# State-space scan of a hybrid decoder step: decay differences by one 48-row product, step sizes folded into the inputs, fills placed by hand

## The reference

```python
cum = cumsum(dt * a)                              # per head, within the block (a < 0)
seg = cum[i] - cum[j]                             # per head, i >= j
lmat = where(mask, exp(where(mask, seg, 0)), 0)
cb = einsum('bign,bjgn->bgij', C, B)
scores = cb * lmat * dt[j]
y = einsum('bghij,bjghp->bighp', scores, x) + einsum(C, state) * exp(cum)[..., None]
wts = exp(cum[last] - cum) * dt
state = state * exp(cum[last]) + einsum('bjgn,bjgh,bjghp->bghpn', B, wts, x)
```

## Time and profile before

| | |
|---|---|
| median of three executions | 3562.12 us |
| profiled execution | 3558.76 us, span of the core 3557.2 us, mean TensorE clock 0.919 of full |
| TensorE busy | 3054.7 us (86%) |
| VectorE busy | 1840.0 us (52%) |
| ScalarE busy | 1210.5 us (34%) |
| GpSimd busy | 519.1 us (15%) |
| DMA | 448.18 MB, mean 126 GB/s |

### The profile page before, as it was taken

How to read it: one execution, slowest core, us unless ns; L and a number is a source line. 1 busy time by engine, 2 the same in 40 slices (tenths; PEclk the granted TensorE clock), 3 DMA queues, 4 the chain that set the end, 5 groups by cost and what they waited for, 6 DMA issues and landing times. The chain is left out here.

```text
span 3557.2 us, 63864 instructions
## 1 busy us (share of the span) xinstructions
PE 3054.7 (86%) x25660; PEld 2801.4 (79%) x25660; DVE 1840.0 (52%) x2858; ACT 1210.5 (34%) x1641; POOL 519.1 (15%) x339
## 2 busy tenths in 40 slices
PE   8999888877786998799889998888787778987997
PEld 7998788677575988599889897776675758975997
DVE  4435545584565554344344364555854654643443
ACT  4436321132131443244254363111411214432542
POOL 0005510252220000000000055002422100000000
PEclk9999999887897999999999999998877979999998
DMA  4444410333272555344344444002422624553443
GB/s 157 151 128 144 125 49 3 72 122 107 67 272 83 172 172 194 125 130 148 114 138 148 127 144 132 25 24 70 153 68 76 254 105 162 183 172 138 134 148 104
DMA packets 119406, 448.18 MB, mean 126 GB/s; under 512 B 13616, under 2 KB 23888, under 8 KB 111632
## 3 DMA queue, kind: packets, MB, share of 16 engines
q1 hardware_dynamic: 97920, 329.75, 29.2%
q0 software_dynamic: 21264, 115.34, 8.9%
HBM read 397.01 MB, written 48.02 MB: 125 GB/s over the span
## 5 line engine op out<-in xcount | busy, mean ns | idle before, releaser
L842 PE MATMUL gemm_banks<-in_high,w_high 128*128 128x320 f32 (+1 forms) x2864 | 856.4, 314 | 61.9 <-ACT w_high L1406 33.4
L1406 ACT ACTIVATE w_high<-ring 128x1024 fp32r<-128x1024 f32 x598 | 631.8, 1057 | 745.6 <-PE gemm_banks L846 373.9
L843 PE MATMUL gemm_banks<-in_low,w_high 128*128 128x320 f32 (+1 forms) x2864 | 845.0, 310 | 0.0
L1770 DVE TENSOR_TENSOR w_low<-ring,w_high 128x1024 fp32r<-128x1024 f32 x436 | 532.7, 1222 | 497.8 <-ACT w_high L1406 497.7
L842 PEld LDWEIGHTS gemm_banks<-in_high,w_high 128*128 128x128 f32 x2864 | 548.1, 191 | 71.6 <-issue 63.7
L693 POOL TENSOR_TENSOR w_low<-ring,w_high 128x1024 fp32r<-128x1024 f32 x162 | 411.8, 2547 | 1047.6 <-ACT w_high L1406 793.7
L843 PEld LDWEIGHTS gemm_banks<-in_low,w_high 128*128 128x128 f32 x2864 | 548.0, 191 | 2.7
L846 PE MATMUL gemm_banks<-in_high,w_low 128*128 128x320 f32 (+1 forms) x2864 | 475.0, 308 | 6.2 <-POOL w_low L693 4.0
L846 PEld LDWEIGHTS gemm_banks<-in_high,w_low 128*128 128x128 f32 x2864 | 431.4, 189 | 8.9 <-POOL w_low L693 5.4
L899 PE MATMUL gemm_banks<-in_high,w_high 128*128 128x320 f32 x640 | 218.5, 353 | 33.7 <-ACT stage L1474 13.7
L926 PE MATMUL gemm_banks<-act_high,w_high 128*128 128x320 f32 x704 | 215.0, 318 | 3.3 <-DVE arena L1819 3.3
(11 more groups left out here) (381 smaller groups left out, 4297.0 us busy)
## 6 DMA issues: line engine op xcount, KB each, us to landing
ring<-in_w SPq DMA_DIRECT2D x598, 512.0 KB, 3.5
arena<-in_kc POOLq DMA_DIRECT2D x16, 1024.0 KB, 6.5
arena<-in_vc POOLq DMA_DIRECT2D x16, 1024.0 KB, 8.9
out_fill<-stage SPq DMA_DIRECT2D x80, 160.0 KB, 3.9
arena<-out_fill POOLq DMA_DIRECT2D x4, 2560.0 KB, 12.1
arena<-in_ssm POOLq DMA_DIRECT2D x16, 512.0 KB, 10.4
out_s_ssm<-arena POOLq DMA_DIRECT2D x16, 512.0 KB, 7.0
arena<-in_ret POOLq DMA_DIRECT2D x16, 512.0 KB, 24.5
```

Source lines behind the costliest of these rows:

```text
L842: mm(dst, w_high[:, slot, w(k)], in_high[:, k, 0:n], start=(k == 0), stop=False)
L843: mm(dst, w_high[:, slot, w(k)], in_low[:, k, 0:n], start=False, stop=False)
L1406: f(w_high[:, slot], ring[:, s, 0:D], ACT.Copy).then_inc(weights_high, 1)
L1770: tt(w_low[:, slot], ring[:, pos % RING, 0:D], w_high[:, slot].bitcast(F32), ALU.subtract).then_inc(weights_split, 1)
```

## The change

- The decay differences come from one product per quarter, straight into PSUM: the stationary operand `one_cum` has 48 rows (16 of ones, 16 of zeros, 16 with the cumulative decay), and the moving operand `cumd` holds the diagonal in rows 0 to 15 and the negated identity, spread over 128 columns, in rows 32 to 47. The clamp goes from four VectorE instructions to one ScalarE instruction (`Relu` with scale -1, followed by `Exp` with scale -1).
- The step size is multiplied into x (`xdt`) as it is copied from PSUM, on VectorE; the score is then one multiplication over four heads. `xw` too is made straight from PSUM. ScalarE no longer copies x, and copies B instead.
- TensorE's order is new: 4 fills per block instead of 5 (and 4 in the third block as before, between other steps), the read of the state ahead of quarters 2 and 3, the update ahead of the turning back, y turned back into banks 3 and 6. After the blocks, the first sample update, the sum of squares, and then the other sample updates with a fill after each.
- The silu of z moves from ahead of the scan into the third block. The gate comes ahead of the samples' updates, and the final scaling between the fourth and the fifth; the projection for retention waits for the last update instead of `done`. The mask of C for the samples (`Cm`) moves to the end of the second block.
- VectorE prepares `one_cum` by three small instructions during the convolution, and ScalarE writes the negated identity at the head of the scan.

```diff
+        one_cum = dts[0:48, 4]
...
                 for t, b in enumerate(IN_PAIRS):
+                    if t == NS // 2:
+                        pool.wait_ge(ss["V"].sem, ss["V"].value["done"])
+                        pool.dma_start(outs["ssd"], rb).then_inc(dma["ssd_stored"][0], 16)
                     pool.wait_ge(ss["V"].sem, ss["V"].value[("updated", t)])
                     n += save(outs["s_ssm"][l, b], ssS[:, b])
-
-                pool.wait_ge(ss["V"].sem, ss["V"].value["done"])
-                pool.dma_start(outs["ssd"], rb).then_inc(dma["ssd_stored"][0], 16)
...
-                    need(V, "tok") if tb == 0 else need(V, (tb - 1, "state"))
+                    if tb == 0:
+                        need(cv_a, CB - 1)
+                        need(V, "tok")
+                    else:
+                        need(V, (tb - 1, "y"))
...
-                    fill("fill_ssd", 1)
-                    need(V, (tb, "tr"))
...
+
+                def cum(tb, q):
+                    c0, n = TBS[tb]
+                    if q < 2:
+                        need(V, (tb, "cumd"))
+                        need(A, "negated") if tb == 0 else need(V, (tb - 1, "state"))
+                    else:
+                        need(A, (tb, "exp", q - 2))
+                    here = bank(4 + q % 2)[0:n, :].rearrange("p (a b) -> p a b", b=P)[:, :, 0:n]
+                    hit(mm(here, one_cum[:, c0:c0 + n], cumd[0:48, 4 * q:4 * q + 4, 0:n], start=True, stop=True),
+                        M, (tb, "cum", q))
+
+                def y(tb, q):
+                    n = TBS[tb][1]
+                    need(V, (tb, "score", q))
+                    if tb and q == 0:
+                        need(V, (tb - 1, "yf"))
+                    for j in range(4):
+                        hd = 4 * q + j
+                        ins_ = mm(bank((3, 6)[q // 2])[0:n, (hd % 8) * 64:(hd % 8 + 1) * 64], sco[0:n, q % 2, j, 0:n],
+                                  xdt[0:n, hd * 64:(hd + 1) * 64], start=True, stop=True)
+                    hit(ins_, M, (tb, "y", q))
...
+                def update(tb):
+                    n = TBS[tb][1]
+                    need(A, (tb, "exp", 3))
+                    for g in range(2):
+                        ins_ = mm(bank(4 + g)[:, 0:512], btok[0:n, g], xw[0:n, g * 512:(g + 1) * 512],
+                                  start=True, stop=True)
+                    hit(ins_, M, (tb, "update"))
...
-                        ins_ = tr(bank(k // 4)[:, (k % 4) * P:(k % 4) * P + n], ytok[0:n, k * P:(k + 1) * P],
+                        ins_ = tr(bank((3, 6)[k // 4])[:, (k % 4) * P:(k % 4) * P + n], ytok[0:n, k * P:(k + 1) * P],
...
+                fill("fill_ssd", 1)
+                for tb in range(3):
+                    turn(tb)
+                    fill("fill_ssd", 1)
+                    cum(tb, 0)
+                    cum(tb, 1)
+                    fill("fill_ssd", 1)
+                    y(tb, 0)
+                    cum(tb, 2)
+                    y(tb, 1)
+                    cum(tb, 3)
+                    fill("fill_ssd", 1)
+                    read(tb)
+                    y(tb, 2)
+                    y(tb, 3)
                     if tb < 2:
...
+                        update(tb)
+                    fill("fill_ssd", 1)
+                    turn_back(tb)
+                fill("fill_ssd", 1)
+                sample_update(0)
+                fill("fill_ssd", 1)
+                for k in range(KT):
+                    if k == 0:
+                        need(A, "sq")
+                    ins_ = mm(bank(6)[:, 0:T], K("ones"), z[:, k, :], start=(k == 0), stop=(k == KT - 1))
+                hit(ins_, M, "sum")
+                for j in range(1, 4):
+                    sample_update(j)
+                    fill("fill_ssd", 1)
+                fill("fill_ssd", 20 - filled["fill_ssd"])
                 need(V, ("updated", NS - 1))
-                fill("fill_ssd", 20 - filled["fill_ssd"])
-                sums(M, "sum", K("ones"), lambda k: z[:, k, :], T, [(A.sem, A.value["sq"])])
-                need(V, "done")
...
                 silus(1 + CB)
-                arrived(act_, layer, "z_back")
-                A_.mark(f(z, z, ACT.Silu), A, "z")
...
             def ssd():
                 V, A, M = ss["V"], ss["A"], ss["P"]
+                need(cv_v, CB - 1)
+                A_.mark(f(cumd[32:48], each(K("ident", 32, 48)[:, 32:48], P), ACT.Copy, scale=-1.0), A, "negated")
                 fill("fill_ssd", 1)
                 for tb, (c0, n) in enumerate(TBS):
-                    need(M, (tb, "tr"))
-                    A_(f(xtok[0:n, 0:512], bank(0)[0:n, 0:512], ACT.Copy))
-                    A_.mark(f(xtok[0:n, 512:1024], bank(1)[0:n, 0:512], ACT.Copy), A, (tb, "tr"))
                     fill("fill_ssd", 1)
                     for q in range(4):
-                        need(V, (tb, "seg", q))
-                        A_.mark(f(seg[0:n, q % 2, :, 0:n], seg[0:n, q % 2, :, 0:n], ACT.Exp), A, (tb, "exp", q))
-                        if q in (0, 2):
+                        if q == 2:
+                            need(V, (tb, "tr"))
+                            A_.mark(f(btok[0:n], bank(2)[0:n, 0:2 * P].rearrange("p (a b) -> p a b", b=P), ACT.Copy), A, (tb, "tr"))
+                        need(M, (tb, "cum", q))
+                        if q >= 2:
+                            need(V, (tb, "score", q - 2))
+                        here, s = bank(4 + q % 2)[0:n, :].rearrange("p (a b) -> p a b", b=P)[:, :, 0:n], seg[0:n, q % 2, :, 0:n]
+                        A_(f(s, here, ACT.Relu, scale=-1.0))
+                        A_.mark(f(s, s, ACT.Exp, scale=-1.0), A, (tb, "exp", q))
+                        if q % 2:
                             fill("fill_ssd", 1)
-                    fill("fill_ssd", 2 if tb < 2 else 1)
-                fill("fill_ssd", 20 - filled["fill_ssd"])
+                    if tb == 2:
+                        arrived(act_, layer, "z_back")
+                        A_.mark(f(z, z, ACT.Silu), A, "z")
+                    fill("fill_ssd", 1)
+                fill("fill_ssd", 2)
                 need(V, "gate")
                 A_.mark(f(z, xc[:, 0:8], ACT.Square), A, "sq")
                 need(M, "sum")
-                rsqrt(sroot, mp[:, 0, 0:T], sinv, A, "root")
+                rsqrt(sroot, bank(6)[:, 0:T], sinv, A, "root")
+                fill("fill_ssd", 20 - filled["fill_ssd"])
...
+                V_(nc.vector.memset(one_cum, 0.0))
+                V_(nc.vector.memset(one_cum[0:16], 1.0))
+                V_(copy(one_cum[32:48], D_(0)))
...
+                spread(0)
                 V_(nc.vector.memset(sst, 0.0))
-                need(cv_a, CB - 1)
-                for g in range(2):
-                    ins_ = tt(Cm[:, g], rep(xc[:, 10 + g, TP:T], NS), split(K("seqrow"), NS, C64), ALU.mult)
-                    V_(ins_) if g == 0 else V_.mark(ins_, V, "cm")
...
-                    V_.mark(tt(cumd[0:16, :, 0:n], rep(D_(0)[:, c0:c0 + n], 16), each(id16, n), ALU.mult), V, (tb, "cumd"))
...
-                    V_(copy(btok[0:n], bank(2)[0:n, 0:2 * P].rearrange("p (a b) -> p a b", b=P)))
...
-                    need(A, (tb, "tr"))
-                    x3, w3 = (split(v, 16, C64)[0:n] for v in (xtok, xw))
-                    V_.mark(tt(w3, x3, each(tok[0:n, tb, 3], C64), ALU.mult), V, (tb, "tr"))
...
-                        for j in range(4):
-                            ins_ = ts(seg[0:n, q % 2, j, 0:n], bank(4 + q % 2)[0:n, j * P:j * P + n],
-                                      tok[0:n, tb, 0, 4 * q + j:4 * q + j + 1], 0.0, ALU.subtract, ALU.min)
...
+                    heads8 = lambda v: v.rearrange("p (a b) -> p a b", b=C64)
+                    for g in range(2):
+                        V_(tt(heads8(xdt[0:n, g * 512:(g + 1) * 512]), heads8(bank(g)[0:n, 0:512]),
+                              each(tok[0:n, tb, 1, 8 * g:8 * g + 8], C64), ALU.mult))
+                    V_.mark(tt(cbm[0:n, :, 0:n], bank(2)[0:n, 2 * P:4 * P].rearrange("p (a b) -> p a b", b=P)[:, :, 0:n],
+                               rep(K("ssdmask", 0, n) if tb < 2 else K("s_ssdmask", 0, 64), 2), ALU.mult), V, (tb, "tr"))
+                    for g in range(2):
+                        ins_ = tt(heads8(xw[0:n, g * 512:(g + 1) * 512]), heads8(bank(g)[0:n, 0:512]),
+                                  each(tok[0:n, tb, 3, 8 * g:8 * g + 8], C64), ALU.mult)
+                        V_(ins_) if g == 0 else V_.mark(ins_, V, (tb, "xw"))
...
                         need(A, (tb, "exp", q))
                         if q >= 2:
                             need(M, (tb, "y", q - 2))
-                        for j in range(4):
-                            ins_ = stt(sco[0:n, q % 2, j, 0:n], seg[0:n, q % 2, j, 0:n],
-                                       tok[0:n, tb, 1, 4 * q + j:4 * q + j + 1], cbm[0:n, q // 2, 0:n], ALU.mult, ALU.mult)
-                            V_(ins_) if j < 3 else V_.mark(ins_, V, (tb, "score", q))
```

(19 more changed lines are left out.)

179 lines of the change are left out of this document (75 added, 104 removed).

## The result

The changed kernel takes 3436.79 us (median; 3434.59 to 3440.33), the kernel before beside it 3560.43: a ratio of 0.9651, with a 95% interval of 0.9639 to 0.9663. The profiled execution took 3440.33 us (span 3438.8, mean clock 0.934 against 0.919), against the 3428.6 that the prediction's sum gave for it.

A forecast was written before the change was run, and what follows sets the result against it. The scan was taken to be bound by TensorE's gaps and the low clock after them. Head 10.0, blocks 58.6 and 30.5, tail 52.1 sum to 151.2 us against 219.3; less 3 for `ret`, 130 saved: 3432 us, range 3403 to 3490.

The forecast's parts named there:

- The bound: Scan, 219.3 us a layer: TensorE idle 58.6 us in gaps and running at a low clock after them.
- The blocks: Scan's three blocks: TensorE's list without gaps takes 29.3, 29.3 and 30.5 us; before 55.9, 47.7 and 43.1.
- cover of about 1.5 us for score 0: Quarter 0 of a block: score 0 is ready about 1.5 us before the 3.7 us fill ends.
- ScalarE against VectorE for the clamp: Clamp of 512 elements: 0.6 us on ScalarE, 0.7 on VectorE, so level, against the page's rule for VectorE.
- The head: Start of the scan: 10.2 us plus 1.0 for VectorE's small instructions minus 1.2 for `Cm`, 10.0 us.
- The tail: After block three: updates, sum and scaling beside fills, `ret` begins at 52.1 us against 62.4 before.
- `ret`: Stage after the scan: state stores ahead of its weights cost 3 us a layer, bounds -2 and 20.
- The sum: Scan 151.2 us against 219.3; less 3 for `ret`, 65.1 us a layer saved, 130 in all.
- Exposed chains: Rival, chance 0.15: broadcast, clamp, exponential, score lie open in most of 12 quarters; half open 3470 us, far end 3506.
- Starved `ret`: Rival, chance 0.12: stores ahead of weights cost 20 us instead of 3, 34 us for both layers: 3466 us.
- given back: Rival, chance 0.03: retention or the stage's end waits the full 65 us for GpSimd's later stores and loads; no change.
- Low clock throughout: Rival, chance 0.03: short float32 products do not hold 2.4 GHz, scan 292 us against 219, whole 3708 us.

The follow-up runs named there:

- z first: Changed kernel with the silu of z put back ahead of ScalarE's first copy of a fill: 3457.22 us.
- both with the head on ScalarE: Changed kernel with `one_cum` prepared on ScalarE, not VectorE: 3437.33 us; the same plus sum of squares and root ahead of all sample updates: 3391.74 us.
- short splits: Changed kernel with GpSimd splitting only 32 of 1024 columns of the scan's 20 fill chunks: 3412.65 us.
- the interleaved list: Kernels with clamps on VectorE, next quarter's clamp put ahead of this quarter's score: 3478.97 us with four instructions per quarter, 3473.13 with one.
- The early sum: Changed kernel with the sum of squares and root ahead of all sample updates, scaling behind them: 3397.82 us.
- the clamp five times: Changed kernel with ScalarE's `Relu` issued five times per quarter on the same data: 3466.74 us.

## Why the prediction was right

**The bound.** Right: the scan paid for gaps and for the low clock after them. It lost 60.2 us of its 219.3, and in the blocks, where TensorE's list is ready, its clock is 1.00 but for one stretch. That stretch, 3 us at 0.50 in the second block with no gap ahead of it, costs 1.5 us a layer. It is absent in four of the runs (z first, both with the head on ScalarE, short splits); what decides it stays open.

**The blocks.** Forecast 29.3, 29.3 and 30.5 us, measured 28.0, 29.4 and 28.2. The sum leaned high by 3.5 us a layer, as it said it would; the read of the samples alone took 7.06 us where the earlier trace rows had 8.95. The runs bracket the cover of about 1.5 us for score 0: one more clamp hid, four more gave waits of up to 1.7.

**What took the gaps away.** The prediction said that VectorE had the next quarter's clamps ahead of this quarter's scores, and went on to sum without pricing it. That line is the largest part that a run shows. Of 61.1 us a layer in the blocks, the runs show 7.2 for z and 16.7 for the interleaved list (103.9 against 87.2). Two fills moved to the tail are 7.4 by the 3.7 of the earlier trace rows. What is left, 29.8, nearly half, is argued and was not run alone: three waits for the scores of quarter 3 (4.41, 4.41, 4.35) behind ScalarE's copy of a fill would, at the measured 16.7 for 9.0 us of waits, be an estimated 24.5.

**ScalarE against VectorE for the clamp.** The rows were right that the engines are level on this form: 0.59 and 0.60 us on ScalarE, 0.69 on VectorE, and no difference in the whole. Clamp and exponential follow each other with 0.03 us between them and no table load, as "ScalarE: Activation LUTs" (Table sets) in the Trainium skill has it; its rule to use VectorE for relu neither helped nor hurt here.

**The head.** 10.0 forecast, 10.81 measured: the last filter, which falls into the head, lay beside a split and took 3.95 us instead of 1.80; with the splits short it took 1.86 and the head 9.92. (In the second layer it took 3.95 us in both kernels.) Another 1.3 us lie ahead of the head in the convolution, 0.9 of them VectorE's three instructions (the run without them there). ScalarE's first copy came at 798.26 and not near 795.

**The tail.** This is the term that was mis-sized: 52.1 forecast, 62.65 measured. The three waits stand where they were forecast (2.3, 3.8 and 2.9 us), but are 4.61, 3.70 and 6.32. The step that failed is the pricing of VectorE's operations by their lone rows: gate 2.8, first mask 0.6 and scaling 4.7 took 3.36, 2.69 for two masks, and 6.68 beside the splits that the fills bring with them, and the update's first half 3.27 instead of 1.2. The prediction had named this contention for the scores and forgotten it in the tail, where it lies on the path. With the splits short the tail is 52.4. Part of the price comes by the clock: after the waits of 4.61 and 6.32 us it was 0.50 and an update took some 3.7 us; after 2.11 and 2.26, with the splits short, it took about 2.0. The early sum shows the other remedy: it leaves the operations drawn out and takes them off the path.

**`ret`.** 3 us more were forecast, 0.35 less were measured. The stores did go ahead of its weights: two chunks came late, by 6.39 us (963.44) and 7.33 (990.22). TensorE waited 0.61 and 1.55 us for them, no more. Retention's loads were issued at 976.88, some 30 us after the start of `ret` as against 1 before; retention's first products waited 2.25 us in both kernels. The delay, 30 us where about 23 were forecast, was harmless, as forecast.

**The sum.** Per layer: head +0.8, blocks -3.5, tail +10.55, `ret` -3.35, convolution +1.3, in all 5.8 more; twice that is the 11.7 us between 3428.6 and 3440.33. So the small miss is partly luck: an error of 10.55 us was met by two of the other sign. The median lies 3.5 below the profiled execution, where the prediction had added 3.4, so the miss of the median is 4.8.

**The rivals.** Exposed chains: no wait of TensorE for scores over 0.2 us was left. Starved `ret` and given back: see above. Low clock throughout: the clock is 1.00, 0.94 and 1.00 in the blocks and 0.84 in the tail.

## What to carry to other kernels

Before counting instructions on an engine with a hand-written order, ask of each waiting instruction what stands behind it: one clamp ahead of a ready score cost 33 us of 3440, whether it was one instruction or four. Price a wait of TensorE above its length where the work behind it is dense: here 16.7 us for 9.0, 12.2 for 5.0 with the clamp five times, and 8.8 for the single 6.76 of z. And price VectorE's operations on the path by their rows beside GpSimd's work, not by their lone ones. When a gain is found, look at the tail again: the best order put the sum of squares, on which a long serial chain hangs, ahead of all work that does not need it.

## What the runs showed of the hardware

GpSimd's splits draw out more than VectorE's two-input instructions. Two masks of 64x256 with one data input took 2.69 us beside a split and 0.73 without; three filter steps 3.95 and 1.80; a 128x1024 multiplication 3.27 and 1.22; the 2560-element gate 3.36 and 2.82. All but the gate are about 2 us longer whatever their own length, near to the 2.3 to 2.4 us of a split, so it reads as a delay and not as a factor; the gate began when all but 0.7 us of its split were over, and is 0.5 longer. The two instructions of `xw`, which read PSUM, took 1.42 us beside a split (801.73) and 1.42 without. "GPSIMD Engine Reference" (Specifications) in the Trainium skill names two SBUF inputs and a 2-port mode as the cases of contention; by it the masks, with one data input, could only be the latter, and no row tells an instruction's mode.

A copy of a fill, a high part and the next instructions on ScalarE overlap slightly in the rows (878.15 for 1.05 us, the next at 879.10), so a queue on ScalarE is a little shorter than the sum of its durations. The load of a function table ahead of the silu took 1.28 us, and it was hidden in the third block.
